# The forget gates of an HGRN mixer in logarithms, all four heads in turn

## The reference, cut to what matters

```
def gla_chunkwise(q, k, v, log_f):            # chunks of 16 positions
    b = jnp.cumsum(log_f, axis=3)             # along the chunk
    q_dec = q * jnp.exp(b)
    k_dec = k * jnp.exp(-b)
    ...
    k_end = k * jnp.exp(b_last - b)
    chunk_decay = jnp.exp(b_last[:, :, :, 0, :])

log_forget = logaddexp(log1p(-lb) + log_sigmoid(z), log(lb))   # log(lb + (1-lb) sigmoid(z))
k = -expm1(log_forget)                        # = (1-lb) (1-sigmoid(z))
```

## Time and profile before

| | us |
|---|---|
| median of 3 runs | 1974.82 |
| lowest, highest | 1965.98, 1982.25 |
| profiled execution | 1979.54 |
| its span, first to last instruction | 1977.6 |
| TensorE, VectorE, ScalarE, GpSimd busy | 1719.3, 723.8, 388.8, 360.0 |

### The profile page before, as it was taken

One profiled execution on the slowest core, in us unless ns is written; L12 is line 12 of the kernel. 1 busy time (PEld: TensorE's weight loads), 2 busy tenths in 40 slices (PEclk: granted clock), 3 DMA queues, 4 the chain that ended last, 5 costly groups with the idle time before them and its releaser, 6 DMA issues. The chain is left out here.

```text
span 1977.6 us, 20206 instructions
## 1 busy us (share of the span) xinstructions
PE 1719.3 (87%) x8104; PEld 921.8 (47%) x8104; DVE 723.8 (37%) x1077; ACT 388.8 (20%) x649; POOL 360.0 (18%) x401
## 2 busy tenths in 40 slices
PE   6996898987999999998379769999789999999972
PEld 3552666655444444443135437665554444444420
DVE  2388756634121111111224887556431111111113
ACT  2223354020111111110112332640201111111101
POOL 1177357000000000000112762660000000000001
PEclk9997789987999999999789976899789999999996
DMA  8000110440999999999720002005229999999995
GB/s 362 1 0 11 62 57 1 117 171 30 418 428 428 428 428 427 429 428 427 306 116 1 0 11 96 22 1 172 116 100 427 427 429 429 427 427 429 429 427 184
DMA packets 58545, 475.88 MB, mean 241 GB/s; under 512 B 18032, under 2 KB 18032, under 8 KB 31664
## 3 DMA queue, kind: packets, MB, share of 16 engines
q1 hardware_dynamic: 45616, 448.39, 54.5%
q10 hardware_dynamic: 10528, 17.76, 2.4%
q0 software_dynamic: 2304, 8.39, 1.2%
HBM read 448.55 MB, written 23.86 MB: 239 GB/s over the span
## 5 line engine op out<-in xcount | busy, mean ns | idle before, releaser
L776 PE MATMUL bank<-ring,hbuf 128*64 128x512 f32 x1024 | 458.0, 601 | 42.0 <-DMA ring<-wu 40.6
L777 PE MATMUL bank<-ring,hbuf 128*64 128x512 f32 x1024 | 459.2, 602 | 0.0
L1545 DVE COPY raw<-bank 128x256 f32<-128x256 f32 x64 | 27.2, 425 | 777.2 <-PE bank L792 777.2
L776 PEld LDWEIGHTS bank<-ring,hbuf 128*64 128x64 f32 x1024 | 138.3, 139 | 333.5 <-issue 331.3
L768 PE MATMUL bank<-raw,hbuf 128*128 128x256 f32 x1024 | 239.9, 389 | 15.4 <-DVE raw L1501 15.4
L1757 POOL DMA_INDIRECT hbuf<-expert_rows,dest_i x16 | 15.5, 971 | 1272.1 <-ACT small L1086 1267.8
L806 PE MATMUL bank<-ring,raw 128*64 128x512 f32 x512 | 233.4, 599 | 5.2 <-DVE raw L1545 5.2
L497 PE MATMUL bank<-hbuf,ring 128*128 128x512 f32 x480 | 217.7, 615 | 19.1 <-DVE raw L1112 15.3
L808 PE MATMUL bank<-ring,raw 128*64 128x512 f32 x512 | 233.5, 599 | 0.0
L768 PEld LDWEIGHTS bank<-raw,hbuf 128*128 128x128 f32 x1024 | 192.6, 193 | 44.9 <-DVE raw L1501 15.6
L497 PEld LDWEIGHTS bank<-hbuf,ring 128*128 128x128 f32 x480 | 94.3, 198 | 138.0 <-issue 138.0
(11 more groups left out here) (331 smaller groups left out, 2157.2 us busy)
## 6 DMA issues: line engine op xcount, KB each, us to landing
ring<-wg SPq DMA_DIRECT2D x64, 2048.0 KB, 18.4
ring<-wu SPq DMA_DIRECT2D x64, 2048.0 KB, 22.7
ring<-wd SPq DMA_DIRECT2D x64, 2048.0 KB, 20.7
ring<-w_in SPq DMA_DIRECT2D x8, 2048.0 KB, 20.6
expert_rows<-raw ACTq DMA_DIRECT2D x128, 128.0 KB, 8.8
ring<-w_out SPq DMA_DIRECT2D x4, 2048.0 KB, 10.4
expert_rows<-raw SPq DMA_DIRECT2D x7, 512.0 KB, 24.0
gain_rows<-gains SPq DMA_DIRECT2D x5, 512.0 KB, 11.3
```

Of the source, the lines that this page charges most:

```text
L776: mm(pb[2 + par][0:CAP, :], tokens[:, k, :], W_gate[par][:, k, :], start=(k == 0), stop=(k == KT - 1))
L777: last = mm(pb[2 + par][CAP:P, :], tokens[:, k, :], W_up[par][:, k, :], start=(k == 0), stop=(k == KT - 1))
```

## The change

ScalarE now does the sigmoid as well: per head exp(-z), then ln(1 + exp(-z)), then exp of minus that; then ln(scale * s + bias) is the logarithm of the gate. VectorE sums it along chunks with the two scans, whose first operand is a constant tile (`chunk_on`, 0 where a chunk starts, 1 elsewhere). ScalarE takes exp of the sum and of its negative. So both reciprocals, the clamp, the add, the affine step and GpSimd's split go. The clamp moves into the evacuation of z (max with -69), and the evacuations of groups 9 and 11 move to VectorE. Each head has scratch tiles of its own (`h_s`, `h_l`), and all four heads go through each step before the next one, before any rope work. The tanh of the two q silus is written into `q_dec[0]` and `q_dec[2]`, that of the g silus into `h_s`, and the latter come after rope tile 3. `rope_rstd` takes tiles in batches (0 and 1, 2 and 3, 4): the Ln of a batch, then the Exp. TensorE's rope waits for the Ln (`r_ln`) of the tile two earlier, not its Exp; the scores of head 0 too.

```diff
-        ht_e, ht_s, ht_k, ht_f, ht_d0, ht_d1, ht_F, ht_R = (ring[:, 5, 512 * i:512 * i + 512] for i in range(8))
+        h_s = [ring[:, 5, 512 * i:512 * i + 512] for i in range(HG)]
+        h_l = [ring[:, 5, 2048 + 512 * i:2560 + 512 * i] for i in range(HG)]
+        by_chunk = lambda ap: ap.rearrange("p (c t) -> p c t", t=CH)
...
+        def by_vector(n):
+            return n % 2 == 0 or 8 <= n < 12
         def wait_evacuated(engine, n):
-            if n % 2 == 0:
-                engine.wait_ge(s["ev_d"], n // 2 + 1)
-            else:
-                engine.wait_ge(s["ev_a"], n // 2 + 1)
+            done = sum(by_vector(m) == by_vector(n) for m in range(n + 1))
+            engine.wait_ge(s["ev_d" if by_vector(n) else "ev_a"], done)
...
@@ tensor_program, rope(j) and hgrn_in(0)
-                    pe.wait_ge(s["r_rs"], j - 1)
+                    pe.wait_ge(s["r_ln"], j - 1)
...
@@ scalar_program
-            for n in range(9, 14, 2):
-                evacuate(n)
-            jobs = [hq[0], hq[1]] + Z + hg
-            def sig_exp(j):
-                n = {0: 12, 1: 13, 2: 8, 3: 9, 4: 10, 5: 11, 6: 20, 7: 21}[j]
+            def gate_exp(hh):
+                wait_evacuated(act, 8 + hh)
+                A(Z[hh], Z[hh], ACT.Exp, scale=-1.0).then_inc(s["h_e"], 1)
+            def gate_sigmoids():
+                act.wait_ge(s["h_e"], HG)
+                for hh in range(HG):
+                    ins = A(h_s[hh], Z[hh], ACT.Ln, bias=1.0)
+                link(ins)
+                for hh in range(HG):
+                    A(h_s[hh], h_s[hh], ACT.Exp, scale=-1.0).then_inc(s["h_s"], 1)
+            def gate_log(hh):
+                act.wait_ge(s["h_s"], hh + 1)
+                A(h_l[hh], h_s[hh], ACT.Ln, scale=lbs[:, 16 + hh:17 + hh], bias=lbs[:, 12 + hh:13 + hh]).then_inc(s["h_l"], 1)
+            def gate_decay(hh):
+                act.wait_ge(s["h_c"], hh + 1)
+                A(h_l[hh], h_s[hh], ACT.Exp)
+                A(h_s[hh], h_s[hh], ACT.Exp, scale=-1.0).then_inc(s["h_f"], 1)
+            def silu_tanh(to, z, n):
                 wait_evacuated(act, n)
-                if j:
-                    act.wait_ge(s["sig_r"], j)
-                if 2 <= j < 6:
-                    A(ht_e, jobs[j], ACT.Exp, scale=-1.0).then_inc(s["sig_e"], 1)
-                else:
-                    A(ht_e, jobs[j], ACT.Tanh, scale=0.5).then_inc(s["sig_e"], 1)
+                A(to, z, ACT.Tanh, scale=0.5).then_inc(s["sig_e"], 1)
             def q_copies(p):
@@ -905,37 +919,43 @@
                     act.wait_ge(s["pe"], 16)
                 A(rope_sq[j], rope_x[j], ACT.Square).then_inc(s["r_sq"], 1)
-            def rope_rstd(j):
-                act.wait_ge(s["r_pe"], j + 1)
-                link(A(rope_sq[j], R_BANK[j % 2][0][:, :], ACT.Ln, bias=eps, scale=1.0 / HD))
-                A(rope_sq[j], rope_sq[j], ACT.Exp, scale=-0.5).then_inc(s["r_rs"], 1)
-            sig_exp(0)
-            sig_exp(1)
+            def rope_rstd(first, last):
+                for j in range(first, last):
+                    act.wait_ge(s["r_pe"], j + 1)
+                    A(rope_sq[j], R_BANK[j % 2][0][:, :], ACT.Ln, bias=eps, scale=1.0 / HD).then_inc(s["r_ln"], 1)
+                act.wait_ge(s["r_ln"], last)
+                for j in range(first, last):
+                    A(rope_sq[j], rope_sq[j], ACT.Exp, scale=-0.5).then_inc(s["r_rs"], 1)
+            for hh in range(HG):
+                gate_exp(hh)
+            gate_sigmoids()
+            silu_tanh(q_dec[0], hq[0], 12)
+            evacuate(13)
+            for hh in range(HG):
+                gate_log(hh)
+            silu_tanh(q_dec[2], hq[1], 13)
+            for hh in range(HG):
+                gate_decay(hh)
             q_copies(0)
             q_copies(1)
             evacuate(15)
-            sig_exp(2)
             rope_square(0)
             evacuate(17)
-            sig_exp(3)
             rope_square(1)
             rope_square(2)
             evacuate(19)
             rope_square(3)
             rope_square(4)
-            sig_exp(4)
-            rope_rstd(0)
+            rope_rstd(0, 2)
             evacuate(21)
-            sig_exp(5)
-            rope_rstd(1)
             evacuate(23)
-            rope_rstd(2)
-            sig_exp(6)
-            rope_rstd(3)
+            rope_rstd(2, 4)
             evacuate(25)
-            rope_rstd(4)
-            sig_exp(7)
+            act.wait_ge(s["head"], HG)
+            silu_tanh(h_s[0], hg[0], 20)
+            silu_tanh(h_s[1], hg[1], 21)
+            rope_rstd(4, 5)
...
@@ vector_program
-                V.tensor_copy(to, of).then_inc(s["ev_d"], 1)
+                if 8 <= n < 12:
+                    TS(to, of, -69.0, None, ALU.max).then_inc(s["ev_d"], 1)
+                else:
+                    V.tensor_copy(to, of).then_inc(s["ev_d"], 1)
...
-            evacuate(10)
+            evacuate(9)
             dve.wait_ge(s["den"], 1)
             V.reciprocal(pv_den, pv_den).then_inc(s["inv"], 1)
+            evacuate(10)
+            evacuate(11)
...
-            def sigmoid(j):
-                dve.wait_ge(s["sig_e"], j + 1)
-                link(TS(ht_s, ht_e, 1.0, None, ALU.add))
-                link(V.reciprocal(ht_s, ht_s))
-            def silu(j, z, count):
-                dve.wait_ge(s["sig_e"], j + 1)
-                STT(out=z, in0=ht_e, scalar=1.0, in1=z, op0=ALU.add, op1=ALU.mult).then_inc(s["q_silu"], 1)
-                dve.wait_ge(s["q_silu"], count)
-                V.memset(small[:, 60:61], 0.0).then_inc(s["sig_r"], 1)
-            def gate_chain(hh):
-                one_less = lbs[:, 16 + hh:17 + hh]
-                bound = lbs[:, 12 + hh:13 + hh]
-                dve.wait_ge(s["sig_e"], 3 + hh)
-                link(TS(ht_e, ht_e, 1.0e30, None, ALU.min))
-                sigmoid(2 + hh)
-                if hh:
-                    dve.wait_ge(s["f_split"], hh)
-                link(TS(ht_f, ht_s, one_less, bound, ALU.mult, ALU.add))
-                V.memset(small[:, 61:62], 0.0).then_inc(s["f_ready"], 1)
-                link(STT(out=ht_k, in0=ht_e, scalar=one_less, in1=ht_s, op0=ALU.mult, op1=ALU.mult))
-                V.memset(small[:, 60:61], 0.0).then_inc(s["sig_r"], 1)
-                dve.wait_ge(s["f_split"], hh + 1)
-                V.tensor_tensor_scan(out=ht_F[0:HD, :], data0=ht_d0[0:HD, :], data1=ht_d1[0:HD, :], initial=0.0,
+            def silu(t, z, count):
+                dve.wait_ge(s["sig_e"], count)
+                STT(out=z, in0=t, scalar=1.0, in1=z, op0=ALU.add, op1=ALU.mult).then_inc(s["q_silu"], 1)
+            def gate_k(hh):
+                dve.wait_ge(s["h_s"], hh + 1)
+                if hh == 0:
+                    dve.wait_ge(s["pe"], KT + 1)
+                STT(out=k_dec[hh], in0=Z[hh], scalar=lbs[:, 16 + hh:17 + hh], in1=h_s[hh],
+                    op0=ALU.mult, op1=ALU.mult).then_inc(s["h_k"], 1)
+            def gate_sum(hh):
+                dve.wait_ge(s["h_l"], hh + 1)
+                dve.wait_ge(s["h_k"], hh + 1)
+                to, of, on = h_s[hh], h_l[hh], cst("chunk_on")
+                V.tensor_tensor_scan(out=to[0:HD, :], data0=on[0:HD, :], data1=of[0:HD, :], initial=0.0,
                                      op0=ALU.mult, op1=ALU.add)
-                link(V.tensor_tensor_scan(out=ht_F[HD:P, ::-1], data0=ht_d0[HD:P, ::-1], data1=ht_d1[HD:P, ::-1],
-                                          initial=0.0, op0=ALU.mult, op1=ALU.add))
-                V.tensor_copy(dec_n[0:HD, :], ht_F[0:HD, CH - 1::CH])
-                V.tensor_copy(dec_n[HD:P, :], ht_F[HD:P, 0::CH])
-                V.tensor_copy(dec_s[hh][0:HD, :], ht_F[0:HD, CH - 1::CH])
-                V.tensor_copy(dec_s[hh][HD:P, :], ht_F[HD:P, 0::CH])
-                link(V.reciprocal(ht_R, ht_F))
-                V.memset(dec_s[hh][:, 0:1], 0.0)
-                V.memset(dec_s[hh][:, NCH - 1:NCH], 0.0)
+                V.tensor_tensor_scan(out=to[HD:P, ::-1], data0=on[HD:P, ::-1], data1=of[HD:P, ::-1], initial=0.0,
+                                     op0=ALU.mult, op1=ALU.add).then_inc(s["h_c"], 1)
+            def decayed(hh):
+                dve.wait_ge(s["h_f"], hh + 1)
+                F, R = h_l[hh], h_s[hh]
+                V.tensor_copy(dec_n[0:HD, :], F[0:HD, CH - 1::CH])
+                V.tensor_copy(dec_n[HD:P, :], F[HD:P, 0::CH])
+                link(TT(k_dec[hh], k_dec[hh], R, ALU.mult))
                 V.memset(dec_n[0:HD, NCH - 1:NCH], 0.0)
                 link(V.memset(dec_n[HD:P, 0:1], 0.0))
-                if hh == 0:
-                    dve.wait_ge(s["pe"], KT + 1)
-                link(TT(k_dec[hh], ht_k, ht_R, ALU.mult))
-                TT(k_end[hh].rearrange("p (c t) -> p c t", t=CH), k_dec[hh].rearrange("p (c t) -> p c t", t=CH),
-                   dec_n[:, :, None].broadcast_to([P, NCH, CH]), ALU.mult)
+                TT(by_chunk(k_end[hh]), by_chunk(k_dec[hh]), dec_n[:, :, None].broadcast_to([P, NCH, CH]), ALU.mult)
```

(52 more changed lines are left out.)

## The result

| | before | after |
|---|---|---|
| median, us | 1977.21 (4 runs) | 1925.32 (4 runs) |
| lowest, highest | 1965.98, 1982.25 | 1919.32, 1927.34 |
| profiled execution | 1979.54 | 1919.32 |
| its span | 1977.6 | 1917.5 |

The ratio is 0.974, with a 95% interval of 0.969 to 0.979: 52 us faster. In a second set of runs the same kernel took 1924.17 (median of 5) against 1979.41 (11 runs of before), a ratio of 0.971 [0.969, 0.974]: 55 us. The prediction was 1920, a gain of 55, in a range of 1904 to 1945.

What follows compares the result with a forecast made beforehand. VectorE's gate chains set the pace while TensorE waits; the stage's end moves 27.2 us per layer, plus 0.3 for the clock. Twice 27.5 is 55 off 1979.5, 1924.5, or 1920 by the median; range 1904 to 1945.

Steps and rivals of the forecast that it cites:

- TensorE runs through: Layer 1, from 126.7 to 157.9: TensorE works without a gap; three waits (20.8 us) and the slow stretches go.
- The heads: VectorE's four heads ahead of the rope work: about 3.3 us each, head 0 done at 89.2, head 3 at 99.
- cover: Between rope tile 0's gain ready at 100.3 and TensorE wanting it at 102.5: 2.2 us; beyond, each us costs TensorE one.
- The tail of rope: ScalarE's last rope work: tanh, loads, Ln, Exp; GpSimd's spread v starts at 163.8, before 191.01, gaining 27.2 us per layer.
- The moment given for layer 2: Sign to look for: the rope 4 products of layer 2 run near 1114 (1166.7 less 27.5 less 25.7).
- GpSimd free in time: GpSimd's rotations and powers, 73.4 us from 81.9, end at 155.3, leaving 8.5 us of slack before its spread v.
- rival 2: GpSimd late, or VectorE late through it, 18%: GpSimd ends at 175.8, time 1945; or heads stretch, 1932.
- The clock bonus: First k v products behind the spread v may run at 2.4 GHz: nothing to 3 us per layer, 0.3 taken.
- Rival 3: The clock pays more, 8%: 3 us per layer in HGRN stage, another 1 to 3 in rope and score products: 1908.
- The sum: Both layers: 2 x 27.5 = 55 us off the profiled 1979.5, giving 1924.5; 1920 against the median of 1974.8.

## Why the prediction was right, step by step

**TensorE runs through: right.** The predicted order of ends and the measured one differ by the 2.6 us that this execution's groups are earlier (79.30 against 81.88), and by little else: rope 2 was put at 126.7 and ran at 123.94, rope 4 at 157.9 and ran at 154.92. No wait is left on the path that the three waits held.

**The heads: right, their cover 0.9 us too small.** VectorE after (L1201 is a head's q_dec, head 0 and head 3; L1206 the gain of rope tile 0):

```profile
85.67 0.69 DVE L1201 TENSOR_TENSOR qd<-qd,ring 128x512 f32<-128x512 f32 x1 [3.69 <-ACT qd L913]
...
95.83 0.69 DVE L1201 TENSOR_TENSOR qd<-qd,ring 128x512 f32<-128x512 f32 x1
...
97.16 0.48 DVE L1206 TENSOR_SCALAR raw<-raw,pack_sb 128x512 f32<-128x512 f32 x1
```

"The first head's q_dec waits for all eight" q copies: it waits 3.69 us for them. The last head is done at 96.5 (at 99.1 in the second profile, whose groups start when they did before), against 99. The gained tile is there at 97.6, and here the prediction misread who waits for it: it let rope 0 wait as a whole, at 102.5, but only its second product reads the gained tile. That one starts at 100.76, so the cover is 3.1 us, predicted 2.2. The run with the reciprocals given back shows that this cover is real and thin.

**The tail of rope: right.** ScalarE after:

```profile
156.77 1.28 ACT L925 ACT_TABLE_LOAD   x1
158.07 0.69 ACT L925 ACTIVATE ring<-bank,consts_sb 128x512 f32<-128x512 f32 x1
158.78 1.28 ACT L928 ACT_TABLE_LOAD   x1
160.07 0.63 ACT L928 ACTIVATE ring<-ring 128x512 f32<-128x512 f32 x1
```

Each load takes 1.28 us and the next instruction starts 0.01 to 0.02 us behind it. The Trainium skill ("ScalarE: Activation LUTs", What ACT_TABLE_LOAD costs) budgets 2.66 us for a switch, a drain included; these rows don't agree with the drain, and the term of the sum (1.3 each) held. The spread v was put at 163.8; it starts at 161.66 in an execution that is 2.6 us early, and at 164.28 in the second profile of the same kernel, whose groups start when they did before: 26.7 us of gain per layer, predicted 27.2. Layer 2 repeats it: from the start of group 16 to the spread v takes 82.36 us in both layers of the first profile (79.30 to 161.66, 1031.66 to 1114.02), 109.1 in both layers of before. The moment given for layer 2 was off: its rope 4 products were put near 1114 and ran at 1107.27, and at 1109.73 in the second profile, because executions differ outside this stage too (below).

**GpSimd free in time: right, and the term too large.** I had it end at 155.3; it ended at 146.8. Started at 79.59, its chain took 67.2 us instead of 73.4. The 73.4 came from a chain that VectorE disturbed; with VectorE's heads done at 96.5 and much idle time behind, fewer of GpSimd's operations were stretched (its 128x2048 multiply took 5.45 us instead of 6.44). So rival 2 was farther off than its 18% suggest: the slack was 14.8 us, not 8.5. In the kernel without reciprocals, though, where the splits stayed, GpSimd did become the end of the stage.

**The clock bonus: wrong, and small.** I gave 0.3 us per layer to a first k v product at full clock. Two took 2.05 us at 162.85, the slow level, behind the idle of 2.79; the evacuation of the k v products starts 29.39 us earlier than before, the spread v 29.35. Nothing came. The stage behind went at 0.71. Rival 3, a bonus of 3 us per layer, has nothing for it in the rows.

**The sum.** Twice 26.7 is 53.4, and the medians say 52 and 55. The predicted 55 contained 0.6 for the clock and 0.5 per layer too much elsewhere. Nothing finer can be told, because single executions differ by more outside the stage. From the spread v of layer 1 to the first transposes of layer 2 they took 809.0 us (before), 807.5 and 804.6 (the two profiles of the changed kernel); 3.0 us of the last are one group of 64 products (L745, now L749) that took 12.15, 12.18 and 9.17 us at a granted clock of 0.58, 0.58 and 0.78. From the spread v of layer 2 to the end they took 803.5, 803.5 and 809.4. The 1920 itself is 4 to 5 us under both medians for another reason: it was counted from the 1974.8 of three runs, and the later sets of before gave 1979.7 and 1979.4.

**What the experiments add.** That the waits were "queued behind a gate chain" was read right, but the trace of before doesn't tell how the gain divides between reciprocal and split. By duration the reciprocals seemed the larger part (6.70 against 2.4 us per head). On the chip each is worth 22 us alone and the two 49.5 together.

## What to carry to other kernels

When one in-order queue has two delays in series, one of them a wait for another in-order queue, taking out the larger one alone can bring much less than expected (22 us here where I had said 45): the queue becomes faster, meets the other engine at a busier moment, and that engine's own end becomes the bound. Price such a removal by the time at which each next consumer wants its operand, and write the cover down (here 3.1 us) beside the gain, taken at the very instruction that waits; then a later edit of one instruction of 3.35 us per head can be seen to cost some 22 us. After a change that moves a stage's end, read who releases the new end: here a buffer shared with the last rope tile, and a ScalarE copy queued behind it, worth another 10 us.

## What the runs showed of the hardware that I had not expected

**A one-input VectorE operation held for the whole of a GpSimd one.** In the kernel without the split, GpSimd's 128x2048 multiply and VectorE's clamp of 128x512, which takes 0.43 us elsewhere:

```profile
130.52 5.83 POOL L1651 TENSOR_SCALAR ring<-ring,consts_sb 128x2048 f32<-128x2048 f32 x1
```

```profile
131.07 5.56 DVE L1159 TENSOR_SCALAR ring<-ring 128x512 f32<-128x512 f32 x1
```

VectorE ends at 136.63, 0.28 us behind GpSimd's 136.35. I had reckoned with stretches of 1 to 2 us; the price here is what is left of the other engine's instruction, so wide GpSimd operations are the expensive ones. The kernel with neither repeats it with another one-input operation (the gain of a rope tile, 4.95 us at 137.85, ending 0.28 us behind GpSimd's multiply of 5.76). For a scan, which has two inputs, the remainder was too high a price: in the kernel before one took 4.50 us from 168.09 and ended 0.66 us ahead of GpSimd's 6.44 from 166.81. The Trainium skill ("SBUF — State Buffer", Who interferes with whom) calls the shared port pair an exclusive lock held for the instruction; the two one-input rows agree, and the scan's end ahead of GpSimd's does not (by 0.66 us, and the profile's ends for GpSimd are rough).

**The same kernel starts at two clocks.** In windows of 2 us early in the first projection group, TensorE's granted clock (the number ahead of the DMA share), in the profile of after and in the second profile of the same kernel:

```profile
26.00:28.00 2.00, 2.00 (x6) 0.80 (x6) 0.40 (x3) 1.41 (x3) 0.00 (x0) 1.00 0.96 410
```

```profile
26.00:28.00 2.00, 2.00 (x3) 0.67 (x2) 0.40 (x3) 1.18 (x1) 0.00 (x0) 0.50 0.96 410
```

The instructions are the same and the idle time ahead of the group too (1.90 us); one execution goes at 2.4 GHz and one at 1.2, and before went at 0.50 there as well. From the first product of this group to group 16 took 55.31 us in the first profile (23.99 to 79.30) and 57.01 in the second (24.92 to 81.93). The other 0.9 us of the 2.6 come ahead of it: the 32 transposes in front took 5.36 us in one and 6.18 in the other. Of the ten profiles of this study six show 1.00 in this window and four 0.50, and the four are of different kernels (before, the kernel with neither, the one with the reciprocals given back, and the second of the changed kernel). In layer 2 the first profile has the faster start again: from the first transposes to group 16 it takes 62.5 us, before 65.0, the second profile 65.2. That is some 5 us of the 60 between the two profiled executions, and a reason to set a predicted moment against the start of its own stage before calling it missed. What decides the level in an execution stays open; no run varied it.
